# A mixture-of-experts decoder layer: weighting the experts' rows as they leave PSUM and adding them to the tokens by accumulating DMAs

## The reference

```python
u = rmsnorm(h, g_ffn)
g_idx = argmax(group_logits)                 # one of 4 groups
top_v, top_i = top_k(within, 2)              # two of its 8 experts
w_sel = softmax(top_v) * p_sel
y = zeros_like(u)
for e in range(32):
    hid = silu(u @ w1[e]) * (u @ w3[e])      # 1024 -> 256
    y = y + combine[:, e:e + 1] * (hid @ w2[e])   # 256 -> 1024
return h + y
```

## Time and profile before

| | us |
|---|---|
| median of 3 runs | 633.73 |
| lowest and highest | 631.4 and 635.51 |
| the profiled execution, its own time | 632.39 |
| its span in the trace | 630.7 |

### The profile page before, as it was taken

How to read it: one execution, slowest core, us unless ns; L and a number is a source line. 1 busy time by engine, 2 the same in 40 slices (tenths; PEclk the granted TensorE clock), 3 DMA queues, 4 the chain that set the end, 5 groups by cost and what they waited for, 6 DMA issues and landing times.

```text
span 630.7 us, 9237 instructions
## 1 busy us (share of the span) xinstructions
PE 599.2 (95%) x3575; PEld 412.6 (65%) x3575; DVE 249.2 (40%) x577; ACT 229.2 (36%) x435; POOL 138.8 (22%) x229
## 2 busy tenths in 40 slices
PE   8899999998999997999999999999999999878896
PEld 8788778895666564566788756656656655545554
DVE  3654154323563875378473772111111111101217
ACT  6816424343464454576344632212212212111220
POOL 8100001120133332234310102232232232222110
PEclk9799899999999999899999999999999999989999
DMA  8920000007000064000379498999999999999995
GB/s 250 389 86 1 0 2 0 1 1 274 11 2 0 1 266 141 4 1 1 141 289 409 195 377 349 364 388 398 379 387 393 380 392 393 396 391 400 400 386 213
DMA packets 32364, 139.54 MB, mean 221 GB/s; under 512 B 8624, under 2 KB 10720, under 8 KB 19264
## 3 DMA queue, kind: packets, MB, share of 16 engines
q1 hardware_dynamic: 25440, 124.92, 51.3%
q0 software_dynamic: 6304, 11.93, 5.6%
q10 hardware_dynamic: 576, 2.10, 0.8%
HBM read 130.75 MB, written 16.06 MB: 233 GB/s over the span
## 4 chain that ended last, share of the span: by engine, by line
PE 81%; DVE 10%; issue 3%; DMA 2%; ACT 2%; SPq 0%; DVEq 0%; ACTq 0%
PE ps L2222 18%; PE ps L1873 15%; PE ps L2253 9%; PE ps L2060 6%; PE ps L1949 5%; PE ps L2004 5%; PE ps L2180 5%; PE ps L2049 5%; PE ps L2238 2%; DMA w_in_ffcq<-in_w_in 2%; PE ps L2024 2%; PE ps L1846 1%; PE ps L1809 1%; PE ps L2099 1%; DVE sums_s L1630 1%
## 5 line engine op out<-in xcount | busy, mean ns | idle before, releaser
L2222 PE MATMUL ps<-w,xt 128*64 128x256 f32 x1024 | 118.2, 384 | 12.4 <-issue 12.1
L2222 PEld LDWEIGHTS ps<-w,xt 128*64 128x64 f32 x1024 | 77.9, 138 | 59.5 <-issue 30.1
L1562 DVE TENSOR_TENSOR xt<-ps,g_ffn_c 128x512 f32<-128x512 f32 x32 | 22.0, 691 | 185.9 <-PE ps L2180 185.9
L2253 PE MATMUL ps<-w,hT 128*64 128x512 f32 x256 | 61.8, 604 | 0.0
L1241 ACT ACTIVATE hsb<-ps,row_scale 128x256 f32<-128x256 f32 x32 | 15.2, 475 | 112.6 <-PE ps L2222 112.6
L879 POOL DMA_INDIRECT xg<-h_rows,idx x30 | 28.8, 961 | 108.9 <-PE ps L2180 108.6
L871 POOL DMA_INDIRECT y_rows<-yh,idy x29 | 29.4, 1015 | 64.3 <-ACT yh L1263 64.3
L809 POOL TENSOR_SCALAR_AFFINE_SELECT probT<-probT 128x128 f32<-128x128 f32 (+2 forms) x80 | 23.5, 312 | 90.1 <-ACT probT L1158 89.4
L2060 PE MATMUL ps<-probT,vals 128*128 128x512 f32 (+4 forms) x160 | 42.6, 410 | 0.0
L2049 PE MATMUL ps<-qT,kT 68*128 68x400 f32 (+9 forms) x160 | 42.2, 408 | 0.0
L1640 DVE TENSOR_REDUCE nmax<-ps 128x1 bf16<-128x528 f32 (+1 forms) x64 | 28.0, 500 | 25.2 <-PE ps L2025 25.2
(11 more groups left out here) (340 smaller groups left out, 1001.7 us busy)
## 6 DMA issues: line engine op xcount, KB each, us to landing
w<-in_w SPq DMA_DIRECT2D x96, 1024.0 KB
y_rows<-zeros POOLq DMA_DIRECT2D x1, 4096.0 KB, 12.3
yg<-y_rows SPq DMA_DIRECT2D x4, 1024.0 KB, 11.7
x<-in_x SPq DMA_DIRECT2D x4, 512.0 KB, 5.4
w_in_v<-in_w_in SPq DMA_DIRECT2D x1, 2048.0 KB, 10.4
w_in_k<-in_w_in SPq DMA_DIRECT2D x1, 2048.0 KB, 16.0
w_in_q<-in_w_in SPq DMA_DIRECT2D x1, 2048.0 KB, 20.8
w_oa<-in_w_o SPq DMA_DIRECT2D x1, 2048.0 KB, 10.3
```

The costliest lines, as they stand in the source:

```text
L2222: ins = pe.matmul(ps[j * slots:(j + 1) * slots, 2 + b, 0:F], xt[b][:, k, :], w13[s][:, j, k, :], start=(k == 0), stop=(k == DK - 1))
L2253: ins = pe.matmul(ps[q * slots:(q + 1) * slots, 6 + b, :], hT[b][:, m, :], w2s[s][:, m, q * 512:(q + 1) * 512], start=(m == 0), stop=(m == ...
```

## The change

1. ACT copies the products of the sent experts with a scale, `slot_coef[:, e]`, so the rows in `y_rows` are weighted already. For this `slot_coef` has a column for all 32 experts: `all_coef` (128 x 4 x 2 x 32) takes the place of `kept_coef` (128 x 4 x 2 x 3), and the matmuls that turn it get 32 columns instead of 3. The copy of the first expert waits for `tables_read`, the signal that `slot_coef` is made.
2. SP's loads of `yg` go. POOL, behind its last scatter and the branch, waits for the scatters and issues eight DMAs that add rows of `y_rows` to x in SBUF (`accum_op=ALU.add`), 128 rows of 4 KB each: first row k=0 of the four tiles, and then row k=1 of each, which waits for the first of its tile (`pair_in[t]`).
3. DVE's `add_rows` goes, PE's `combine_loaded` and POOL's `coef_diag` too. DVE's `add_kept(t)` waits for both DMAs of its tile and for PE's sum.
4. In the branch for overfull experts the coefficient is gathered per slot too and used as a scale (`coef_rows`, `fb_coef`). `first_slots`, two instructions on POOL or DVE, waits on the engine's own step counter instead of a semaphore `first_part`.

The core of the diff:

```diff
-BY_PE = [(NT - 2, 1), (NT - 1, 0), (NT - 1, 1)]
...
-        slot_coef = place("slot_coef", [P, KEPT], F32, r_tri + 480)
-        kept_coef = late_new("kept_coef", [P, NT, 2, KEPT])
+        slot_coef = place("slot_coef", [P, NE], F32, r_tri + P * 4)
+        all_coef = place("all_coef", [P, NT, 2, NE], F32, r_s)
...
+        pair_in = [sem(f"pair_in{t}") for t in range(NT)]
...
-            for b in range(2):
-                sp.wait_ge(y_stored[b], 16 * ((SENT + 1 - b) // 2))
-            for t in range(NT):
-                sp.dma_start(yg[t][:, :, :], y_tiles[t]).then_inc(tile_in[t], 16)
             for t in range(NT):
                 sp.wait_ge(out_made, t + 1)
                 sp.dma_start(out_tiles[t], x[:, t, :]).then_inc(out_stored, 16)
...
-            for n, (t, k) in enumerate(BY_PE):
-                pool.wait_ge(h13_done, SENT - 1)
-                pool.tensor_scalar(coef_diag[n][:, :], ident[:, :], coef[:, t, k:k + 1], None, ALU.mult
-                                   ).then_inc(diag_made, 1)
-
             pool.wait_ge(over_made, 1)
...
+            for b in range(2):
+                pool.wait_ge(y_stored[b], 16 * ((SENT + 1 - b) // 2))
+            for k in range(2):
+                for t in range(NT):
+                    if k:
+                        pool.wait_ge(pair_in[t], 16)
+                    pool.dma_start(x[:, t, :], y_tiles[t][:, k, :], accum_op=ALU.add).then_inc(pair_in[t], 16)
...
-                act.activation(yh[b][:, :], ps[:, 6 + b, :], ACT.Copy).then_inc(y_copied, 1)
+                if e == 0:
+                    act.wait_ge(tables_read, 1)
+                act.activation(yh[b][:, :], ps[:, 6 + b, :], ACT.Copy, scale=slot_coef[:, e:e + 1]).then_inc(y_copied, 1)
...
-            dve.tensor_tensor(kept_coef[:, :, :, :], ehots[:, :, :, SENT:],
-                              coef[:, :, :].unsqueeze(3).to_broadcast([P, NT, 2, KEPT]), ALU.mult
+            dve.tensor_tensor(all_coef[:, :, :, :], ehots[:, :, :, :],
+                              coef[:, :, :].unsqueeze(3).to_broadcast([P, NT, 2, NE]), ALU.mult
                               ).then_inc(coefs_made, 1)
...
-            def add_rows(t, parts=2):
-                dve.wait_ge(tile_in[t], 32)
-                for k in range(parts):
-                    step(dve.scalar_tensor_tensor(out=x[:, t, :], in0=yg[t][:, k, :], scalar=coef[:, t, k:k + 1],
-                                                  in1=x[:, t, :], op0=ALU.mult, op1=ALU.add))
-
             def add_kept(t):
+                dve.wait_ge(pair_in[t], 32)
                 dve.wait_ge(combined, t + 1)
                 dve.tensor_tensor(x[:, t, :], x[:, t, :], pair(2 * t, D), ALU.add).then_inc(out_made, 1)
...
-            add_rows(0)
-            add_rows(1)
-            add_rows(2, 1)
...
-                        ins = pe.matmul(ps[:, COUNT, NE:NE + KEPT], slot_hot[:, t, k, :], kept_coef[:, t, k, :],
+                        ins = pe.matmul(ps[:, COUNT, NE:2 * NE], slot_hot[:, t, k, :], all_coef[:, t, k, :],
...
-            combine_loaded(0).then_inc(combined, 1)
-            combine_loaded(1)
-            combine_loaded(2).then_inc(combined, 1)
+                ins = combine(NT - 1, k)
+            ins.then_inc(combined, 1)
```

More of the change, by code:

```diff
@@ L250, in build @@
         r_moe = r_u + 512
-        yg = [place(f"yg{t}", [P, 2, D], F32, ring + 8192 * t if t < NT - 1 else r_moe) for t in range(NT)]
         assert r_qk + 2 * SLOT <= r_moe
@@ L398, in build @@
         zeros = place("zeros", [P, D], F32, ring + SLOT)
-        coef_diag = [place(f"coef_diag{n}", [P, P], F32, r_moe + 8192 + 512 * n) for n in range(len(BY_PE))]
         fb_pair = new("fb_pair", [slots, 1], I32)
         fb_idx = new("fb_idx", [slots, 1], I32)
+        fb_coef = place("fb_coef", [slots, 1], F32, r_tri + P * 4 + NE * 4)
         most = new("most", [P, 1])
@@ L858, in _ @@
             for p in range(LAST):
-                first_slots(pool, p)
+                first_slots(pool, step, p)
             pool.wait_ge(idx_made, 1)
@@ L930, in _ @@
                         ).then_inc(fb_xg, 16)
+                        pool.indirect_dma_start(
+                            out=fb_coef[:, :], out_offset=None, in_=coef_rows,
+                            in_offset=bass.IndirectOffsetOnAxis(ap=fb_pair[:, :].bitcast(U32), axis=0),
+                            bounds_check=2 * SEQ - 1, oob_is_err=False
+                        ).then_inc(fb_xg, 16)
                         pool.wait_ge(fb_act_step, n * 2)
@@ L1256, in store_rows @@
                     k = e - SENT
-                    act.activation(y_hi[k][:, :], ps[:, 6 + b, :], ACT.Copy, scale=slot_coef[:, k:k + 1]
+                    act.activation(y_hi[k][:, :], ps[:, 6 + b, :], ACT.Copy, scale=slot_coef[:, e:e + 1]
                                    ).then_inc(y_copied, 1)
@@ L1290, in _ @@
                         act.wait_ge(fb_pe_step, n * 3)
-                        act.activation(ysb[:, :], pair(4, D)[0:slots, :], ACT.Copy).then_inc(fb_act_step, 1)
+                        act.activation(ysb[:, :], pair(4, D)[0:slots, :], ACT.Copy, scale=fb_coef[:, :]
+                                       ).then_inc(fb_act_step, 1)
         @block.vector
@@ L1694, in _ @@
             positions(LAST)
-            first_slots(dve, LAST)
+            first_slots(dve, step, LAST)
             dve.wait_ge(first_done, 2)
@@ L1740, in split_rows @@
                 dve.wait_ge(y_copied, e + 1)
-                dve.scalar_tensor_tensor(out=y_lo[k][:, :], in0=ps[:, 6 + e % 2, :], scalar=slot_coef[:, k:k + 1],
+                dve.scalar_tensor_tensor(out=y_lo[k][:, :], in0=ps[:, 6 + e % 2, :], scalar=slot_coef[:, e:e + 1],
                                          in1=y_hi[k][:, :].bitcast(F32), op0=ALU.mult, op1=ALU.subtract
@@ L1750, in _ @@
                     dve.wait_ge(coefs_turned, 1)
-                    dve.tensor_copy(slot_coef[:, :], ps[:, COUNT, NE:NE + KEPT]).then_inc(tables_read, 1)
+                    dve.tensor_copy(slot_coef[:, :], ps[:, COUNT, NE:2 * NE]).then_inc(tables_read, 1)
                 if SENT - 2 <= e < NE - 2:
@@ L2304, in _ @@
                         pe.sem_inc(waits_ended, 1)
-            def combine_loaded(n):
-                t, k = BY_PE[n]
-                pe.wait_ge(diag_made, n + 1)
-                pe.wait_ge(tile_in[t], 32)
-                for q in range(2):
-                    ins = pe.matmul(ps[:, 2 * t + q, :], coef_diag[n][:, :], yg[t][:, k, q * 512:(q + 1) * 512],
-                                    start=False, stop=(n != 1))
-                return ins
             def combine(t, k):
@@ L2322, in combine @@
                                         start=(k == 0 and n == 0),
-                                        stop=(k == KEPT - 1 and n == 1 and t < NT - 2))
+                                        stop=(k == KEPT - 1 and n == 1))
                 return ins
@@ L2331, in _ @@
             pe.wait_ge(y_split, KEPT)
-            for t in range(NT - 2):
+            for t in range(NT - 1):
                 combine(t, KEPT - 1).then_inc(combined, 1)
-            combine(NT - 2, KEPT - 1)
             for k in range(KEPT):
-                combine(NT - 1, k)
-            combine_loaded(0).then_inc(combined, 1)
-            combine_loaded(1)
-            combine_loaded(2).then_inc(combined, 1)
+                ins = combine(NT - 1, k)
+            ins.then_inc(combined, 1)
 _INS = ['x', 'meta_tokens', 'g_attn', 'w_in', 'b_f', 'g_fox_q', 'g_fox_k', 'g_q_lat', 'w_uq', 'g_kv_lat', 'w_ukv',
```

23 lines of the change are left out of this document (12 added, 11 removed).

## The result

| | before | after |
|---|---|---|
| median of 20 runs each | 633.81 us (631.40 to 639.27) | 639.22 us (636.72 to 645.53) |
| ratio of the two, 95% interval | | 1.0095 (1.008 to 1.011) |
| profiled execution | 632.39 us | 640.64 us |
| its span | 630.7 us | 639.0 us |
| mean granted TensorE clock | 0.982 | 0.968 |

What follows compares the result with a forecast made beforehand. DVE's chain was taken to bound the end; with the accumulates, 606.5 + 1.3 + 20.6 + 0.5 = 628.9, plus 0.1, 1.2 and 3.6, gives span 633.8, 3.1 us longer, median 636.8 us. Range 628.5 to 650.

Steps and rivals of the forecast that it cites:

- What bounds the end: After the last product: DVE's chain sets the end now; after the change, the movement of y ends last.
- The price of eight transfers, twice the plain rate: POOL's eight accumulating DMAs at the end: reading y and x takes twice 10.3, 20.6 us; chance 0.36 as the forecast.
- A (plain rate): Eight accumulates at the end go at the plain rate: x complete at 618.6, span 626.0, median 629.0; chance 0.18.
- B (1.5 times): Eight accumulates at the end, all bytes counting alike: x complete at 623.8, span 628.7, median 631.7; chance 0.14.
- C (slower than its reads): POOL's DMA queue: engines hold packets until old x returns; at three times, span 644.1, median 647.1; chance 0.28.
- Tile 0 of k=0 lands near 610.9: First accumulate's landing: 606.5 + 1.3 + 2.6 + 0.5, for data start, weights in front, transfer and tail.
- The end of the queue: Behind the accumulates: the other three adds are done before the last tile's, and 3.6 us is for the store.
- The start: POOL's first accumulate issue, behind the last scatter issued at 598.01: 604.90 plus 0.09 for a slower ACT copy, 605.0.
- The last add to the end: From DVE's last add to the end of the span: 3.6 us for the store, as before.
- The waits between the rounds: POOL's k=1 DMAs waiting for k=0: cost nothing, as the other three k=0 transfers keep the engines busy to 618.1.
- The loop's edits: Experts' loop: scaled copies' 2.6 us hidden in ACT's 46.4 us idling; wider coefficient matmuls 0.1 us, let go in rounding.
- Rival D: Experts' loop: scaled copies or wider coefficient matmuls delay it by up to 2.6 us on top, 639.4; chance 0.04.

Runs made afterwards that it cites:

- e1_plain: Changed kernel with plain copies in place of the eight accumulating DMAs, same rows, queue and waits; 630.81 us, ratio 0.9956 to the kernel before.
- e9_late: Changed kernel with POOL also waiting, ahead of the first accumulating DMA, until the last expert's w2 has landed; 644.60 us, ratio 1.0181 to the kernel before.
- e2_hold: Changed kernel with all four of SP's stores held until DVE's last add; 642.07 us, ratio 1.015 to the kernel before.
- e5_nowait: Changed kernel with the k=1 rows accumulated onto other SBUF tiles, without the wait for the first round; 639.94 us, ratio 1.0116 to the kernel before.
- e4_six: Changed kernel with the second (k=1) accumulating DMA of tiles 0 and 1 left out; 637.53 us, ratio 1.0063 to the kernel before.
- e3_scaled: Kernel before with only the scaled copies and wider coefficients; SP loads rows, DVE and PE add them unweighted; 633.18 us, ratio 1.0015 to the kernel before.

## Where the prediction was right and where it was wrong

I forecast a time that a measurement can't tell from no change, 3.1 us more; it is 5.4 us more, told apart. Step by step:

- **What bounds the end.** Right. DVE's chain left the path; PE's sums were complete at 622.1 and waited for nothing; x was late for every add.
- **The price of eight transfers, twice the plain rate.** Right. 2.49 us a tile, 211 GB/s for 412; e1_plain removes the adding alone and gains 8 to 9 us. Rivals A (plain rate), B (1.5 times) and C (slower than its reads) fall with the same rows. By the Trainium skill (Collectives: The Full Stack, The bandwidth ceiling: the fold count and why AG ≠ RS ≠ AR) the pace is set by two reads and not by the adding; its 1.93 stands beside 412 / 211 = 1.95 here, for a DMA within one core. The runs show the pace; that reads are its cause they do not show by themselves.
- **"Tile 0 of k=0 lands near 610.9", the step that failed.** In my sum the first tile was to land 5.9 us after the first issue (605.0 to 610.9): 1.5 of lead, 1.3 for the rest of a weight load, 2.6 of transfer and 0.5 of tail. It takes 7.4 us, so 1.5 us of the miss are there. On idle engines it takes 7.1, where my terms without the weights give 4.6 (e9_late). The lead that I took from a DMA that writes a constant to DRAM is borne out: the engines start 1.6 us after the issue. Wrong was to charge the first tile with the transfer of one tile, 2.6 us, at the full pace from its first byte. The engines are at work for 5.5 us before it lands, slowly at first, and by then have moved 0.95 MB, nearly two tiles. The weight load's 1.3 us was of the right order, 0.9 at the last landing.
- **The end of the queue, the second term.** I had the stores of tiles 0 to 2 in the sum only as 3.6 us behind the last add. They are issued from 627.19 on and take part in the engines' time while the last accumulate runs. From the first landing to the last it is 19.4 us for the 18.0 of my sum, 1.4 more, and holding the stores back gives as much (e2_hold). Before, they had the engines to themselves.
- **The start.** I let POOL's first issue follow the last scatter's by 7.0 us; it is 7.86, 0.9 more: the scatter lands 7.55 us after its issue and POOL needs 0.31 more.
- **The last add to the end.** 3.6 us forecast, 3.0 measured (635.98 to 639.0), 0.6 in my favour.

From the scatter's issue to the end I had forecast 633.8 - 598.01 = 35.8 us; it is 38.9. The four terms together are 1.5 + 1.4 + 0.9 - 0.6 = 3.2, against a miss of 3.1; the rest is rounding. On the medians the miss is 2.3 (5.4 for 3.1).

- **The waits between the rounds.** Right that they cost nothing (e5_nowait), and e4_six shows what they cost once the cover is gone.
- **The loop's edits.** Right: nothing (e3_scaled). Rival D falls.

The range held the time. My chance for a slowdown sat almost wholly on rival C, that is on the rate. The doubled rate gave the 3.1 us that I forecast; what came on top is from the two terms at either end of the eight transfers, to which I had given no spread at all.

It stays open what the accumulate does in its first 4 us: the traces show that few bytes move behind the issue, and not why. A single accumulate with nothing queued behind it and a plain DMA of POOL's from DRAM on idle engines would tell how much of the 7.1 us is sharing and how much the adding; no run here tried them. A kernel that issues the accumulates in front of the last expert's scatter was not tried, since rows of that expert may belong to any token.

## What to carry to other kernels

An accumulating DMA moves the addition off VectorE but, in these runs, doubles the transfer's time on the DMA engines; the place for it is where these engines have that time to spare and nobody waits for the first tile. The time between the first issue and the first landing is paid once however well the rest is pipelined: take it from a row of the same kind, with as many DMAs queued behind it, or give it a range. And work that looks like load may be the cover of a wait: taking out two of the eight DMAs gave 1.7 us on the medians, 3.2 between first issue and last landing, instead of 5.

## What the runs showed of the hardware that was not expected

- An accumulating DMA of 128 rows of 4 KB, DRAM to SBUF: 2.49 us behind others of its kind (plain: 1.3), 7.1 us from issue to landing on idle engines with three more issued behind it (e9_late), issue on POOL 0.84 us (plain 0.53). Four issued in a row overlap on POOL and take 3.64 us together, each row between 0.99 and 1.84 long.
- Stores issued at 627.19 beside accumulates hardly raise the rate: it stays at 205 to 217 GB/s until 631 and only then goes to 344. The stores of the changed kernel land 2.6 to 6.9 us after their issues.
- A 128x1024 f32 addition with both inputs in SBUF takes 3.1 to 3.3 us on POOL, and one of DVE's issued while POOL's runs 3.3 too; DVE alone needs 1.22.
